# Gate products by halves, small loads behind a broadcast, and five transposes in place of fifteen

## The reference, cut to what matters

```python
z = x @ w_in
q, k, v, o, gi, gf, u, ga, gb = jnp.split(z, cuts, axis=-1)
li = gi + b_gate[:H]
lf = jax.nn.log_sigmoid(gf + b_gate[H:])
# for each chunk of tokens
b = jnp.cumsum(lf, axis=-1)
d = where(causal, b[:, None] - b[None, :] + li[None, :], -inf)
m_t = maximum(b + m_prev, max(d, -1))
qk = (q @ k.T) * exp(d - m_t)
h = (s_inter * (q @ c_prev) + qk @ v) / maximum(abs(den), exp(-m_t))
```

## Time and profile before

| | |
|---|---|
| median of three runs | 920.99 us |
| lowest and highest of them | 919.57 and 921.68 us |
| the profiled execution's own time | 921.98 us |
| its span, first to last instruction | 920.6 us |
| mean granted TensorE clock in it | 0.982 |
| TensorE busy | 884.5 us, 96% of the span |
| VectorE busy | 587.3 us, 64% |
| ScalarE busy | 391.3 us, 43% |
| GpSimd busy | 87.2 us, 9% |

### The profile page before, as it was taken

The page is one execution under the profiler, slowest core; times in us unless marked ns, Lnnn a source line. Parts: engine busy times, 40 slices in busy tenths (PEclk is TensorE's granted clock), DMA queues, the critical chain, the costliest instruction groups (busy, mean ns, idle before and its releaser), DMA issues.

```text
span 920.6 us, 14525 instructions
## 1 busy us (share of the span) xinstructions
PE 884.5 (96%) x6007; PEld 787.5 (86%) x6007; DVE 587.3 (64%) x825; ACT 391.3 (43%) x410; POOL 87.2 (9%) x88
## 2 busy tenths in 40 slices
PE   6999999999999999999999999999999999999975
PEld 6998888988889999999999996878888788778841
DVE  3735554745575371233233447899999999999946
ACT  4422132211432332322223104677777677777712
POOL 3000000000000001000101011301110011110043
PEclk8999999999999999999999998999999999999987
DMA  9784083483816042321322915799999999999657
GB/s 300 231 318 110 30 262 105 134 256 102 281 58 206 1 152 92 92 89 54 98 82 99 384 50 213 279 376 381 414 389 392 384 413 401 380 414 379 257 165 173
DMA packets 82212, 207.08 MB, mean 225 GB/s; under 512 B 4222, under 2 KB 57174, under 8 KB 69225
## 3 DMA queue, kind: packets, MB, share of 16 engines
q1 hardware_dynamic: 74184, 177.30, 53.4%
q0 software_dynamic: 7968, 28.93, 9.2%
HBM read 174.68 MB, written 33.76 MB: 226 GB/s over the span
## 4 chain that ended last, share of the span: by engine, by line
PE 74%; DVE 16%; issue 4%; ACT 3%; DMA 2%; POOL 0%; SPq 0%; DVEq 0%; ACTq 0%
PE psum L452 21%; PE psum L454 20%; PE psum L453 20%; DVE split_lo L1467 7%; PE psum L1908 2%; DVE last_lo L1467 2%; PE psum L1918 2%; PE psum L2131 2%; PE psum L1947 1%; DVE xgl L1627 1%; DMA xn<-in_x_prompt_dram 1%; ACT split_hi L1001 1%; PE psum L1933 1%; DVE hs L1636 1%; DVE gs L1633 1%
## 5 line engine op out<-in xcount | busy, mean ns | idle before, releaser
L452 PE MATMUL psum<-x_hi,split_lo 128*128 128x272 f32 x704 | 208.8, 297 | 2.0 <-DVE pbl L1430 1.2
L454 PE MATMUL psum<-x_hi,split_hi 128*128 128x272 f32 x704 | 202.3, 287 | 0.0
L453 PE MATMUL psum<-x_lo,split_hi 128*128 128x272 f32 x704 | 202.1, 287 | 0.0
L1467 DVE TENSOR_TENSOR split_lo<-raw,split_hi 128x2048 fp32r<-128x2048 f32 x72 | 163.3, 2286 | 7.9 <-ACT split_hi L1001 6.9
L1001 ACT CAST split_hi<-raw 128x2048 fp32r<-128x2048 f32 x72 | 137.5, 1912 | 44.1 <-PE psum L454 44.0
L447 DVE TENSOR_TENSOR split_lo<-raw,split_hi 128x2048 fp32r<-128x2048 f32 x35 | 80.0, 2289 | 115.0 <-ACT split_hi L428 114.9
L452 PEld LDWEIGHTS psum<-x_hi,split_lo 128*128 128x128 f32 x704 | 132.6, 188 | 7.3 <-issue 2.7
L453 PEld LDWEIGHTS psum<-x_lo,split_hi 128*128 128x128 f32 x704 | 132.7, 189 | 1.4 <-issue 1.0
L454 PEld LDWEIGHTS psum<-x_hi,split_hi 128*128 128x128 f32 x704 | 132.6, 188 | 0.0
L452 PE MATMUL psum<-split_hi,xgl 128*128 128x512 f32 x192 | 76.3, 398 | 1.3 <-DVE xgl L1627 1.2
L454 PE MATMUL psum<-split_hi,xgh 128*128 128x512 f32 x192 | 74.9, 390 | 0.0
(11 more groups left out here) (383 smaller groups left out, 1753.3 us busy)
## 6 DMA issues: line engine op xcount, KB each, us to landing
raw<-in_w_e_gate_dram SPq DMA_DIRECT2D x32, 1024.0 KB, 8.7
raw<-in_w_e_up_dram SPq DMA_DIRECT2D x32, 1024.0 KB, 8.6
raw<-in_w_e_down_dram SPq DMA_DIRECT2D x32, 1024.0 KB, 8.2
raw<-in_w_in_dram SPq DMA_DIRECT2D x26, 1024.0 KB, 5.6
cb<-in_state_C_dram SPq DMA_DIRECT2D x8, 1024.0 KB, 7.5
out_dram<-cb SPq DMA_DIRECT2D x8, 1024.0 KB, 5.8
y_slots<-ys POOLq DMA_DIRECT2D x15, 512.0 KB, 8.0
kv<-kv_rows SPq DMA_DIRECT2D x4, 1028.0 KB, 8.0
```

Source lines behind the costliest of these rows:

```text
L452: nc.tensor.matmul(out, a_lo, b_hi, start=first, stop=False)
L453: nc.tensor.matmul(out, a_hi, b_lo, start=False, stop=False)
L454: return nc.tensor.matmul(out, a_hi, b_hi, start=False, stop=last)
L1467: v.tensor_tensor(lo, raw2[:, n % MOE_SLOTS, :], hi.bitcast(F32), ALU.subtract).then_inc(w_lo, 1)
```

## The change

There are three edits.

The gate products: the transposes of the last tile go to PSUM banks 2 and 3 instead of 0 and 1 and wait for two tiles of `x_lo` instead of one. G waits for three tiles of `x_lo` and for `wg_lo` before its first half, and for all five tiles before its second half.

The loads: `nn` is issued behind the store of `nm_rows`, and `gain`, `pscale`, `brt` and `wr` behind the broadcast `bm`.

The rows: one tile `turn3` of 68 partitions by 640 columns holds `g_r` on partitions 0 to 3, `em` on 32 to 35 and `w_r` on 64 to 67, with zeros between (a memset at the start). The three copies into `rep4` become one copy inside `turn3`, and the fifteen transposes become five, each of 68 rows. VectorE picks the same 60 columns out of their result.

```diff
+TURNED = 64 + H
...
-    rep4 = keep("rep4", [H, 3, P])
...
-    li, lf, bcum, g_r, m_r, mt, nm, em = lay(r_ht, HT_END, *[(f"row_{n}", [H, N], F32) for n in
-                                             ("li", "lf", "b", "g", "m", "mt", "nm", "em")])
-    w_r = lf
+    li, lf, bcum, m_r, mt, nm, turn3 = lay(r_ht, HT_END, *[(f"row_{n}", [H, N], F32) for n in
+                                           ("li", "lf", "b", "m", "mt", "nm")], ("turn3", [TURNED, SEQ + P], F32))
+    g_r, em, w_r = (turn3[32 * q:32 * q + H, 0:N] for q in range(3))
...
     def startup(i):
 
-        return psum[:, 2 * (i % 4):2 * (i % 4) + 2, :]
+        b = i if i < PT else 1
+        return psum[:, 2 * b:2 * b + 2, :]
...
-            pl.dma_start(nn[:], state_n[0].rearrange("b h d -> (b h) d")).then_inc(nn_in, 16)
+        pl.wait_ge(cst_in, 16)
+
+
+        pl.wait_ge(nm_ok, 1)
+        pl.dma_start(nm_rows, nm[:]).then_inc(nm_out, 16)
+        pl.dma_start(nn[:], state_n[0].rearrange("b h d -> (b h) d")).then_inc(nn_in, 16)
+        pl.wait_ge(nm_out, 16)
+        pl.dma_start(bm[:].rearrange("p h n -> p (h n)"), nm_rows.rearrange("h n -> (h n)").partition_broadcast(P)
+                     ).then_inc(bm_in, 16)
+        with nc.allow_non_contiguous_dma(reason="small parameters"):
             pl.dma_start(gain[:], hn_gain[0].rearrange("h (c p) -> p (h c)", p=P)).then_inc(par_in, 16)
             pl.dma_start(pscale[:], pool_scale[0].rearrange("(g p) -> p g", p=P)).then_inc(par_in, 16)
             pl.dma_start(brt[:], b_router.partition_broadcast(P)).then_inc(par_in, 16)
             pl.dma_start(wr[:], w_router.rearrange("(k p) n -> p k n", p=P)).then_inc(wr_in, 16)
...
-        for q, row in enumerate((g_r, em, w_r)):
-            last = nc.scalar.copy(rep4[:, q, :].rearrange("p (g n) -> p g n", g=4),
-                                  row[:, SEQ:N].unsqueeze(1).to_broadcast([H, 4, NS]))
-        last.then_inc(em_ok, 1)
+        nc.scalar.copy(turn3[:, N:].rearrange("p (g n) -> p g n", g=3),
+                       turn3[:, SEQ:N].unsqueeze(1).to_broadcast([TURNED, 3, NS])).then_inc(em_ok, 1)
...
+        v.memset(turn3[:], 0.0)
...
-        cols = narrow(T_COL)[:, 0:3 * NT * H].rearrange("p (q i h) -> p q i h", q=3, i=NT)
-        v.tensor_copy(col[:], cols).then_inc(t_free[T_COL % 2], 1)
+        cols = narrow(T_COL)[:, 0:96 * NT].rearrange("p (i q c) -> p q i c", i=NT, q=3)
+        v.tensor_copy(col[:], cols[:, :, :, 0:H]).then_inc(t_free[T_COL % 2], 1)
...
-            if i == 4:
-                pe.wait_ge(x_lo_ok, 1)
+            if i == PT:
+                pe.wait_ge(x_lo_ok, 2)
...
-        pe.wait_ge(x_lo_ok, NT)
+        pe.wait_ge(x_lo_ok, 3)
         pe.wait_ge(wgl_ok, 1)
         j = Z["G",]
         z_room(pe, j)
         for a in range(2):
+            if a == 1:
+                pe.wait_ge(x_lo_ok, NT)
...
-        for q, row in enumerate((g_r, em, w_r)):
-            for i in range(NT):
-                at = (q * NT + i) * H
-                src = row[:, i * P:i * P + P] if i < PT else rep4[:, q, :]
-                last = nc.tensor.transpose(narrow(T_COL)[:, at:at + H], src, ident[0:H, 0:H])
+        for i in range(NT):
+            last = nc.tensor.transpose(narrow(T_COL)[:, 96 * i:96 * i + TURNED], turn3[:, i * P:i * P + P],
+                                       ident[0:TURNED, 0:TURNED])
```

More of the change, by code:

```diff
@@ L679, in _ @@
             pl.dma_start(wr[:], w_router.rearrange("(k p) n -> p k n", p=P)).then_inc(wr_in, 16)
-        pl.wait_ge(cst_in, 16)
-        pl.wait_ge(nm_ok, 1)
-        pl.dma_start(nm_rows, nm[:]).then_inc(nm_out, 16)
-        pl.wait_ge(nm_out, 16)
-        pl.dma_start(bm[:].rearrange("p h n -> p (h n)"), nm_rows.rearrange("h n -> (h n)").partition_broadcast(P)
-                     ).then_inc(bm_in, 16)
         pl.wait_ge(ready, H)
```

## The result

| | before | after |
|---|---|---|
| median | 920.89 us (4 runs) | 914.50 us (4 runs) |
| lowest to highest | 919.57 to 921.68 | 913.56 to 915.51 |
| profiled execution's own time | 921.98 | 915.51 |
| its span | 920.6 | 914.3 |
| mean granted clock | 0.982 | 0.986 |

The ratio of the times is 0.9934, with a 95% interval from 0.9919 to 0.9949: the kernel is 6.4 us faster by the medians. In a later session with more runs of both it was 0.9936 (0.9922 to 0.9951). I had forecast 916.9 us and a range down to 915.3, so the direction was right and the size too small.

The account below looks back on a forecast made before the run. TensorE, busy 96% of the span, was taken as the bound. The terms 2.9 + 0.45 + 1.7 = 5.05 us, off the profiled execution's 921.98 us, gave 916.9 us, with a range from 915.3 to 919.4.

Parts of the forecast that it names:

- What bounds the kernel: Whole kernel: TensorE, busy 96% of the span, is the bound, and time won at the start is carried along.
- Edit 1, G by halves: Gate products: G starts at 13.06, the clock is low from 13.65 to 17.06, G ends at 20.5; gain 2.9 us.
- my first rival: Gate products: the clock never falls, queries wait for chunk 0's low split at 19.71; gain 3.7 there, 916.1 us; chance 0.20.
- Edit 2, the loads: Small loads moved later: costed at nothing; earlier weights at the start, a few tenths of a microsecond, put at 0.
- Edit 3, the rows: Row transposes ahead of the value products: five instead of fifteen save 0.45 us, bounds 0.30 to 0.63.
- The second low stretch: Value products behind the transposes: the clock no longer falls, 1.7 us won; called the weakest term.
- The low stretches elsewhere: Rival: low stretches lie elsewhere in other executions, so the second is mostly not there to win; 917.6 us; chance 0.22.
- The clock that keeps its instants: Rival: clock low to 20.48 and again behind the transposes as before; 1.8 us less, 920.2 us; chance 0.10.
- a later wait that takes the gain back: Rival: a later wait, for instance the key products on a weight chunk, takes the gain back; 921 us; chance 0.08.
- the late small loads: Rival: loads behind `bm` land so late that VectorE's copy of the value products is held up; 922.5 us; chance 0.04.

Follow-up runs that it names:

- edits 1 and 3: The changed kernel with the five small loads back at the start: 916.29 us, 4.7 us below the kernel before, ratio 0.9947.
- edit 1 alone: The kernel before with G by halves only, small loads still at the start and fifteen transposes: 916.59 us, ratio 0.9955 to before.
- edit 3 alone: The kernel before with only the fifteen transposes replaced by five of 68 columns: 920.07 us, ratio 0.9986 to before.
- edits 1 and 2: The changed kernel with the fifteen transposes put back: 916.35 us, 4.0 us below the kernel before, ratio 0.9959.
- the filled wait: The kernel before with 18 transposes of 128 columns, never read, in TensorE's wait ahead of G: 0.9 us faster, ratio 0.9984.

## Why the prediction was right or wrong

**What bounds the kernel, right.** TensorE's own time at the start was the path, and what was won there stayed: 6.31 us at the first transpose of the keys, 6.5 us at 539.8, 5.7 us behind the passage to the experts, 6.3 us at the end of the span.

**Edit 1, G by halves: the step that failed.** I wrote that the clock "falls at 13.65", with a low stretch of 3.41 us, and took 2.9 us from this. It never fell in G, in eight traces of eight with edit 1. What showed in its place: with TensorE's idleness ahead of G down from 2.08 us to 0.66, or with the 2.1 us filled by other work, G ran at 2.4 GHz throughout, in 6.0 to 6.1 us. In the first 3.41 us behind the clock's first rise PE was busy for 1.97 us in the earlier trace rows, and for 2.75 us after (11.36 to 14.77). The gain was 4.18 us. That case was my first rival. I gave it 0.20 because part of the work in that stretch was narrow. The start at 13.06 was nearly right: 13.26, since `wg_lo` was finished 0.13 us later in that execution and the weight load came 0.12 us behind it instead of 0.05.

**Edit 2, the loads: the term that was mis-sized, and it set the range.** I put the earlier weights at 0, "a few tenths of a microsecond", and so let the rival end at 19.71, where VectorE had finished the low split of chunk 0. That split came 2.1 us sooner. With edits 1 and 3 only, it does hold up the queries, to 20.39. With a clock that falls nothing at G's end waits for that split; with one that doesn't, it left TensorE idle between two matmuls for 0.45 us with edit 1 alone and for 0.61 with edits 1 and 3: a value that hung on another step's outcome. The medians don't agree on it: added to edit 1 the loads changed 4.4 us into 4.0, added to edits 1 and 3 they changed 4.7 into 6.4. The rest of this step held. `nn` landed at 36.2, 8 us before it was wanted, and the wait for `gain`, `pscale` and `brt` never came to bear.

**Edit 3, the rows.** 0.45 us taken, 0.54 measured for the transposes, within the bounds that I gave (0.30 to 0.63), and 0.09 more from the pause ahead of them, which I had not counted. Five of 68 columns take 0.48 us by their row, of which the last one's own 0.23 is part: they start 0.06 us apart, as those with 4 columns do.

**The second low stretch, right in the trace.** 1.7 us taken, 1.5 measured, and the clock stayed up in eight traces of eight with five transposes. I called it the weakest term; it held, with luck in it: edit 3 alone shows 0.9 us in the medians for this and the shorter transposes together, and the kernel with fifteen transposes and edits 1 and 2 had no such stretch in its trace.

**The sum and its base.** The terms came to 5.05 us, and in the trace were 4.18 + 0.64 + 1.5 = 6.32. The two profiled executions differ by 6.47 us, the medians by 6.4. I had made the sum against the profiled execution's 921.98 us, though it lay 1.0 us above the median, and took the end of my range, 915.3, from that too. From the median of 920.99 that I had, my terms would have given 915.9 us, and the range would have begun at 914.3 and held 914.5. The step on the clock would have been wrong all the same.

**The rivals.** The low stretches elsewhere: in part so, since they vary, but one of 3.4 us or more was in G in all five traces of kernels that wait there for all tiles with nothing to fill the wait, and behind the transposes in five of the six with fifteen. The clock that keeps its instants, a later wait that takes the gain back, and the late small loads: none of them was seen.

**What stays open.** Edits 1 and 2, edit 3 alone and the filled wait show leads at the start that are 1 to 2 us larger than what the medians show. The passage to the experts has a low stretch of 6.8 us in some traces and of 10.2 in others, within one and the same kernel (the changed one has both). Over all kernels it is 10.2 us in six traces of fourteen, in neither of the two of before. It takes 35.40 us in the first trace of before and 36.20 after:

```profile
539.80:575.20 35.40, 33.12 (x330) 28.43 (x329) 22.53 (x51) 11.31 (x10) 4.53 (x3) 0.90 0.41 153
```

```profile
533.30:569.50 36.20, 34.64 (x330) 30.04 (x329) 22.53 (x51) 11.27 (x10) 4.54 (x3) 0.86 0.41 150
```

It is the same work, 330 matmuls, and 0.8 us apart. Which of the two an execution gets was not controlled in any run, and it is as large as several of the effects here. So is what comes behind it: the two profiled executions of the kernel before are 1.1 us apart at 880 us and 2.0 at 900.

## What to carry to other kernels

Here a wait of 2.1 us cost TensorE about as much again in clock (1.9 to 2.5 us, by the filled wait): read the granted clock in the stretches behind each pause and each run of narrow matmuls, and count what a fallen clock costs there along with the pause. When an edit takes a bound away, work out the others anew, since a transfer that nothing waited for may be what is waited for next. Make a sum from a trace, but place it on the median.

## What the runs showed of the hardware

TensorE counts as busy in the narrow transposes, and still its clock fell behind them in five traces of six. In the one trace where eighteen transposes of 128 columns filled the wait, the clock stayed up as it does behind products. With five small loads of 110 KB at the start the low split of the first weight chunk was ready about 2 us later (19.13 to 20.34 in six traces, against 17.36 to 18.43 in the seven with all five behind); 6 KB in 4-byte pieces alone gave 18.86 in one trace. Small loads issued behind a broadcast of 1,088 KB on the same queue began to move when the broadcast's pieces were through, and landed with it or up to 2 us later, not a whole load's time after it: 7.2 to 7.8 us from issue, against 6.1 to 6.7 us for the same four loads at the start.
